# Past keys turned by VectorE in 32x32 blocks and moved by transfers inside the chip, in the attention stage of a decoder step

## What is computed

```python
def stick_breaking(q, k, v, bias, q_offset):
    z = jnp.einsum('bqhd,bkhd->bhqk', q.astype(f32), k.astype(f32)) * (HD_B ** -0.5)
    z = z + bias.astype(f32)[None, :, None, None]
    mask = jnp.arange(Lk)[None, :] < (q_offset + jnp.arange(Lq))[:, None]
    u = jnp.where(mask, jax.nn.log_sigmoid(-z), 0.0)
    rev_excl = lax.cumsum(u, axis=3, reverse=True) - u
    A = jnp.where(mask, jnp.exp(jax.nn.log_sigmoid(z) + rev_excl), 0.0)
    return jnp.einsum('bhqk,bkhd->bqhd', A, v.astype(f32))

past_k = cache_k[page_table].reshape(Bs, -1, H_B, HD_B)
past_v = cache_v[page_table].reshape(Bs, -1, H_B, HD_B)
```

## Time and profile before

| | |
|---|---|
| median of three runs | 1518.87 us |
| profiled execution, its time | 1517.85 us |
| its span | 1516.1 us |
| PE busy over the span | 1463.3 us, 97% |
| DVE, ACT, POOL busy | 75%, 51%, 21% |
| attention stage | from about 794 to 1099 us |

### The profile page before, as it was taken

How to read it: one execution, slowest core, us unless ns; L and a number is a source line. 1 busy time by engine, 2 the same in 40 slices (tenths; PEclk the granted TensorE clock), 3 DMA queues, 4 the chain that set the end, 5 groups by cost and what they waited for, 6 DMA issues and landing times.

```text
span 1516.1 us, 33061 instructions
## 1 busy us (share of the span) xinstructions
PE 1463.3 (97%) x13048; PEld 1391.0 (92%) x13048; DVE 1140.3 (75%) x1855; ACT 776.6 (51%) x1192; POOL 320.0 (21%) x307
## 2 busy tenths in 40 slices
PE   8999999999999999999998888888899999999998
PEld 8999999989999999999997777777699999999998
DVE  7866666668998989889726666666679989899753
ACT  6544444436754636455514555554557546364543
POOL 3000000002322323223141111111243223223221
PEclk9999999999999999999999999999999999999999
DMA  5133333223787786876426554553247777877721
GB/s 189 57 87 86 86 86 86 86 87 93 154 175 166 159 182 149 170 168 147 125 84 210 169 175 162 169 167 112 72 105 153 171 170 157 172 160 163 171 84 63
DMA packets 237716, 205.83 MB, mean 136 GB/s; under 512 B 8268, under 2 KB 224404, under 8 KB 237588
## 3 DMA queue, kind: packets, MB, share of 16 engines
q1 hardware_dynamic: 151346, 147.34, 30.9%
q0 software_dynamic: 68160, 47.20, 20.0%
q10 hardware_dynamic: 18082, 9.48, 2.3%
HBM read 192.19 MB, written 11.80 MB: 135 GB/s over the span
## 4 chain that ended last, share of the span: by engine, by line
PE 88%; DVE 5%; issue 4%; ACT 2%; DVEq 0%; DMA 0%; ACTq 0%
PE acc L2771 21%; PE acc L3095 19%; PE pMO L3095 12%; PE pL L3095 12%; PE acc L3195 5%; PE acc L3032 2%; PE pL L2892 1%; PE acc L3302 1%; PE pMO L3262 1%; PE acc L3318 1%; PE pMO L2961 1%; PE acc L3483 1%; PE acc L3291 1%; DVE pg L2544 1%; PE pMO L3249 1%
## 5 line engine op out<-in xcount | busy, mean ns | idle before, releaser
L654 POOL TENSOR_TENSOR wlo<-wraw,whi 128x512 fp32r<-128x512 f32 x40 | 56.2, 1433 | 455.2 <-ACT whi L768 455.2
L2771 PE MATMUL acc<-xa_hi,whi 128*128 128x288 f32 x544 | 125.2, 311 | 0.6 <-issue 0.6
L854 ACT ACTIVATE hi<-wraw 128x1024 fp32r<-128x1024 f32 x60 | 63.7, 1062 | 106.5 <-DVE wraw L1976 106.2
L2771 PE MATMUL acc<-xa_hi,wlo 128*128 128x288 f32 x544 | 116.6, 296 | 0.0
L837 ACT ACTIVATE hi<-wraw 128x1024 fp32r<-128x1024 f32 x60 | 63.7, 1061 | 102.8 <-PE acc L3095 102.6
L2771 PE MATMUL acc<-xa_lo,whi 128*128 128x288 f32 x544 | 116.2, 295 | 0.0
L3095 PE MATMUL acc<-X_lo,hi 128*128 128x288 f32 x384 | 113.4, 295 | 0.0
L3095 PE MATMUL acc<-X_hi,lo 128*128 128x288 f32 x384 | 113.4, 295 | 0.0
L3095 PE MATMUL acc<-X_hi,hi 128*128 128x288 f32 x384 | 113.2, 295 | 0.0
L1991 DVE TENSOR_TENSOR lo<-wraw,hi 128x1024 fp32r<-128x1024 f32 x60 | 73.4, 1223 | 41.9 <-ACT hi L837 41.9
L3095 PE MATMUL acc<-H_hi,hi 128*128 128x288 f32 x336 | 99.4, 296 | 1.3 <-DVE lo L1997 1.3
(11 more groups left out here) (513 smaller groups left out, 4943.8 us busy)
## 6 DMA issues: line engine op xcount, KB each, us to landing
wraw<-in_w_up_dram SPq DMA_DIRECT2D x64, 512.0 KB, 6.8
wraw<-in_w_down_dram SPq DMA_DIRECT2D x64, 512.0 KB, 6.2
Kp<-in_cache_k_dram SPq DMA_DIRECT2D x32, 512.0 KB, 4.0
Vp<-in_cache_v_dram SPq DMA_DIRECT2D x32, 512.0 KB, 5.6
wraw<-in_w_in_a_dram SPq DMA_DIRECT2D x30, 512.0 KB, 5.1
wraw<-in_w_up_dram POOLq DMA_DIRECT2D x32, 256.0 KB, 4.9
S_even<-in_w_up_dram POOLq DMA_DIRECT2D x32, 256.0 KB, 7.0
S_odd<-in_w_up_dram POOLq DMA_DIRECT2D x32, 256.0 KB, 8.1
```

Source lines behind the costliest of these rows:

```text
L654: ins = pool.tensor_tensor(wlo[s][:, k:k + 2, :], wraw[s][:, k:k + 2, :], whi[s][:, k:k + 2, :].bitcast(F32), ALU.subtract)
L854: act.activation(blocks4(hi31), by_depth(G % 2)[:, 0], ACT.Copy).then_inc(piece_hi, 1)
L2771: last = pe.matmul(acc[a][:, hf, 0:HALF], w[s][:, k, a * P:(a + 1) * P], x[k][:, hf * HALF:(hf + 1) * HALF], start=(k == 0 and n == 0), st ...
```

## The change

PE's `t_fill` and both `t_copy` go. Instead DVE turns a whole page at once in 32x32 blocks, `keys_turned(s, g)`, into a buffer `KX`, one for two pages. A 32x32 block is then still on the wrong 32 partitions; SP puts it right with `keys_moved(s, h)`, 16 transfers from `KX` to `KT` for each half of the past, each of 32 partitions by 512 elements (64 KB). `past_logits` waits for these and reads `KT` in pieces of 32. `keys_turned` for pages 0 and 2 waits until the moves before have landed, since `KX` is one buffer, and `keys_moved` waits until `past_logits` has read the half of `KT`.

The bank `TB` now also takes the transposed values and every second of the transposed weights (`ABANK = [pM, TB, pM, TB, pM]`), `pO` takes the sums and values of the new tokens, which stood in `ZB`. `fg` shrinks to two halves of 512. The order of a turn is written anew on every engine: on ACT `t_copy` drops out, `new_copies` comes after `gates(j, 2)`, `past_gates` and `attn_out` come earlier; SP's loop over j is unrolled. The core of the diff:

```diff
@@ -176,17 +176,19 @@
+                 ("KX", [P, 4, NPAIR, 2, 32], F32)])
         (KT, sgS, fS, pS, ATp, pastO, newE, newO, QB, Oc, kvn, sN, fN, pN, dN, AN, qnew, At0) = arena(
-            xa_at, [("KT", [P, NPAIR, 2, P], F32), ("sgS", [P, 512], F32), ("fS", [P, 512], F32), ("pS", [P, 513], F32),
...
+        N_MOVE = 16 * 16
@@ -525,9 +527,17 @@
                 page = sp.value_load(pt[0:1, bass.ds(4 * s + g, 1)], min_val=0, max_val=cache_k.shape[0] - 1)
-                wait(sp, T_full, 8 * s + 2 * g - 2)
+                wait(sp, k_turned, 4 * s + g - 1)
                 sp.dma_start(Kp[:, g % 2, :], cache_k[bass.ds(page, 1)].rearrange("a p h d -> p (a h d)")
                              ).then_inc(kp_landed[g % 2], 16)
+
+            def keys_moved(s, h):
+
+                sp.wait_ge(k_turned, 4 * s + 2 * h + 2)
+                wait(sp, zS_full, 2 * s + h)
+                for a in range(4):
+                    for b in range(4):
+                        sp.dma_start(KT[32 * b:32 * b + 32, a], KX[32 * a:32 * a + 32, b]).then_inc(k_moved, 16)
@@ -556,15 +566,19 @@
             def pages_and_weights(j, weights, more_pages):
-                kv_store(j)
-                key_page(j + 1, 2)
-                key_page(j + 1, 3)
-                value_pages(j + 1)
                 if more_pages:
                     key_page(j + 2, 0)
                     key_page(j + 2, 1)
+                kv_store(j)
+                keys_moved(j + 1, 1)
+                value_pages(j + 1)
                 if weights:
                     weights(0)
+                if more_pages:
+                    keys_moved(j + 2, 0)
+                    key_page(j + 2, 2)
+                    key_page(j + 2, 3)
+                if weights:
                     weights(1)
@@ -580,13 +594,18 @@
             sp.wait_ge(unit_done, U_OB)
+            keys_moved(0, 0)
             value_pages(0)
+            keys_moved(0, 1)
             key_page(1, 0)
             key_page(1, 1)
+            keys_moved(1, 0)
+            key_page(1, 2)
+            key_page(1, 3)
@@ -2450,8 +2455,19 @@
+            def keys_turned(s, g):
+
+                dve.wait_ge(kp_landed[g % 2], 32 * s + 16 * (g // 2) + 16)
+                if g % 2 == 0:
+                    wait(dve, k_moved, N_MOVE * (2 * s + g // 2))
+                dve.transpose(KX[:, :, :, g % 2, :].rearrange("p b j k -> p j b k"),
+                              Kp[:, g % 2, :].rearrange("p (j b k) -> p j b k", b=4, k=32)).then_inc(k_turned, 1)
+
             dve.wait_ge(n_rs, 2 * n_norm["mix1"] + 2)
             for m in range(NB):
+                if m == NB - 2:
+                    keys_turned(0, 0)
+                    keys_turned(0, 1)
                 dve.wait_ge(unit_done, U_Q + m + 1)
                 dve.tensor_tensor(qT[:, m, :].rearrange(tok2, a=2), accv(m % 2), t2v(rstd), ALU.mult).then_inc(acc_free[m % 2], 1)
                 if m < 4:
@@ -2592,38 +2597,54 @@
-            def pair(j, first):
+            def pair(j, first, more):
                 if first:
                     k_low(0)
                     q_low(0)
+                mask(j, 0)
                 k_rows(j)
-                mask(j, 0)
+                products(j, 0, 0)
+                new_rows(j)
+                new_mask(j)
...
                     past_out_even(0)
                     past_out_odd(0)
-                t_copy(j + 1, 1)
-                new_rows(j)
-                new_mask(j)
-                group(j, 0)
-                past_store(j)
                 mask(j, 1)
+                weights(j, 0, 1)
+                if first:
+                    past_store(0)
+                    keys_turned(1, 2)
+                    keys_turned(1, 3)
                 new_products(j)
-                t_copy(j + 1, 3)
-                queries(j + 1)
-                group(j, 1)
+                products(j, 1, 0)
                 mask(j, 2)
+                products(j, 1, 1)
+                kv_copy(j + 1, 0)
+                weights(j, 1, 0)
+                weights(j, 1, 1)
                 new_out(j)
-                kv_copy(j + 1, 0)
-                t_copy(j + 1, 5)
-                group(j, 2)
-                t_copy(j + 1, 7)
-                k_low(j + 1)
+                for hh in range(2):
+                    products(j, 2, hh)
+                for hh in range(2):
+                    weights(j, 2, hh)
                 past_products(j + 1)
                 past_weights(j + 1)
-                kv_copy(j + 1, 1)
+                if more:
+                    queries(j + 2)
+                    keys_turned(j + 2, 0)
+                    keys_turned(j + 2, 1)
+                k_low(j + 1)
                 q_low(j + 1)
+                if more:
+                    keys_turned(j + 2, 2)
+                    keys_turned(j + 2, 3)
                 past_out_even(j + 1)
                 past_out_odd(j + 1)
+                kv_copy(j + 1, 1)
 
             def ob_low(m):
@@ -2672,18 +2701,22 @@
             kv_copy(0, 0)
+            keys_turned(1, 0)
+            keys_turned(1, 1)
+            dve.wait_ge(row_chain, 3)
+            queries(1)
             past_products(0)
             past_weights(0)
@@ -3264,48 +3301,28 @@
             def past_logits(s, h2):
-                pe.wait_ge(Ta_free, 4 * s + 2 * h2 + 2)
-                pe.wait_ge(Td_free, 4 * s + 2 * h2 + 2)
+                pe.wait_ge(k_moved, N_MOVE * (2 * s + h2 + 1))
                 pe.wait_ge(QB_ready, 4 * s + 4)
-                wait(pe, n_dve, 6 * s)
+                wait(pe, fin_free, 2 * s)
@@ -3331,46 +3348,44 @@
                 if first:
-                    past_values(0)
+                    past_transposed(0)
                 else:
                     past_finish(j)
...
+                if first:
+                    past_values(0)
                 new_rows(j)
+                values_transposed(j)
+                fill(2, 3)
+                logits(j, 1)
                 if first:
+                    fill(3, 4)
                     past_finish(0)
-                t_fill(j + 1, 1)
-                fill(1, 3)
-                values_transposed(j)
-                t_fill(j + 1, 2)
-                logits(j, 1)
-                fill(3, 4)
-                t_fill(j + 1, 3)
+                else:
+                    past_logits(j + 1, 0)
+                    fill(3, 4)
+                fill(4, 5)
+                if first:
+                    past_logits(1, 0)
+                weights_transposed(j, 0)
+                weights_transposed(j, 1)
                 new_sums(j)
-                weights_transposed(j, 0)
-                fill(4, 6)
+                logits(j, 2)
+                fill(5, 8)
+                past_logits(j + 1, 1)
                 new_values(j)
-                weights_transposed(j, 1)
-                logits(j, 2)
-                past_logits(j + 1, 0)
-                t_fill(j + 1, 4)
-                fill(6, 8)
-                t_fill(j + 1, 5)
                 weights_transposed(j, 2)
                 fill(8, 9)
-                t_fill(j + 1, 6)
                 weights_transposed(j, 3)
                 fill(9, 10)
-                t_fill(j + 1, 7)
+                weights_transposed(j, 4)
                 fill(10, 11)
-                past_logits(j + 1, 1)
+                weighted(j)
                 fill(11, 12)
-                weights_transposed(j, 4)
+                past_transposed(j + 1)
                 fill(12, 14)
-                weighted(j)
-                past_transposed(j + 1)
+                past_values(j + 1)
                 fill(14, 16)
-                past_values(j + 1)
 
             def ob_prompt_part(u, k):
```

More of the change, by code:

```diff
@@ L588, in _ @@
             pages_and_weights(0, lambda a: kv_weights(3, a), True)
-            with sp.Fori(1, NPAIR - 3) as j:
+            for j in range(1, NPAIR - 3):
                 pages_and_weights(j, lambda a: kv_weights(j + 3, a), True)
@@ L1386, in new_copies @@
                     act.activation(newE[rows, bass.ds(j, 1), :].rearrange("p a t -> p (a t)"),
-                                   ZB[rows, SMP * hh:SMP * hh + SMP], ACT.Copy).then_inc(n_act, 1)
+                                   pO[rows, SMP * hh:SMP * hh + SMP], ACT.Copy).then_inc(n_act, 1)
             def gates(j, g):
@@ L1394, in gates @@
                     z = pL[:, hh, 0:GW[g]]
-                    act.activation(fg[:, hh, cols], z, ACT.Sigmoid, scale=-SCALE, bias=bias_neg[:, bass.ds(2 * j + hh, 1)]
+                    wait(act, p_done, 6 * j + (2 * g + hh - 1 if g else 0))
+                    act.activation(fg[:, hh, 0:GW[g]], z, ACT.Sigmoid, scale=-SCALE, bias=bias_neg[:, bass.ds(2 * j + hh, 1)]
                                    ).then_inc(s_done, 1)
@@ L2552, in weights @@
                 dve.tensor_tensor(sg[:, hh, cols], sg[:, hh, cols], pg[:, hh, 0:GW[g]], ALU.mult).then_inc(a_done, 1)
-            def group(j, g):
-                for hh in range(2):
-                    products(j, g, hh)
```

(46 more changed lines are left out.)

140 lines of the change are left out of this document (51 added, 89 removed).

## The result

The kernel after takes 1626.78 us (median of 4 runs, 1625.72 to 1627.56) against 1518.72 (4 runs, 1518.13 to 1518.95): ratio 1.0712, interval 1.0693 to 1.0730. Slower, as forecast (0.88), but 49 us beyond the forecast and just past the range's end of 1625. The profiled execution has a span of 1624.7 against 1516.1.

The account below looks back on a forecast made before the run. PE was taken to bound the kernel, holding 88% of the chain. Start +25.6, five turns +35.5 and turn 6 -2.0 gave +59.1 us, so 1578 against a profiled 1517.85 and a median 1.0 above it; range 1532 to 1625.

Parts of the forecast that it names:

- The circle: Attention turn: SP's two move batches, page loads and DVE's turnings lie on PE's path; turn 42.7 against 35.6 us.
- cheap issues: Rival: issues of moves at 0.37 us, everything else as forecast; turn 37.6, total about 1539; chance 0.16.
- a faster kernel: Rival: the moves hold nobody up and PE leads again; 1480 at 0.1 us an issue; chance 0.08.
- small pieces: Rival: transfers in pieces under 2 KB, or not on all DMA engines; about 1690; chance 0.05.
- step 2: Turn: 16 moves and landing, 8.5 + 1.4, to 18.1; PE waits 3.9 before `past_logits(j+1, 1)`.
- Step 5: Turn: 16 moves 8.5 us, first page landed 4.1 later, to 39.5.
- Step 6: Turn: two page turnings 2.4 us and two `past_out` 0.8, to 42.7, the next `past_finish`.
- The clock: PE, once a turn behind the long stop: 3.5 us at half speed lose 1.7; ends nothing and 3.4.
- Step 1: Turn: PE from `past_finish` to the end of `past_logits(j+1, 0)`, 8.2 us including 1.7 for PE's slower clock.
- step 3: Turn: `past_logits` 1.0, `new_values` 0.4, DVE's `new_out` through `past_weights` 2.4 and 2.0; 5.8 us, to 23.9.
- step 4: Turn: `queries` 0.6 us and two page turnings on DVE 2.4, to 26.9.
- dear steps: Rival: turning 2.44 us, page landing 5.6, issue 0.60; turn 51.4, total 1637; chance 0.09.

Follow-up runs that it names:

- the last orders: The orders of `no gaps`, changed against the run with the new start, with two page loads right ahead of each batch of moves: 1515.58 us.
- the last run: `no gaps` with two moves a batch (one on SP, one on POOL) instead of 16, keys on wrong partitions: 1505.12 us, ratio 0.9920.
- no gaps: Against the run with the new start, orders alone: fills ahead of weights_transposed, group 2's weights earlier, start reordered: 1515.58 us, ratio 0.9982.
- the run with the new start: Kernel after with turnings, page loads and moves reordered, eight moves each on SP and POOL, start ordered anew: 1517.73 us, ratio 0.9995.

## Why the prediction was right in its cause and short in its size

The circle was right: both batches of moves lie on PE's path, the waits stand where they were forecast, before `past_finish` and before `past_logits(j+1, 1)`, and the load of page 2 is what DVE waits for. Both waits were larger, 11.7 and 5.5 us where 9 and 4 stood. The turning was right too (1.22 forecast, 1.233 measured), and so were the landing of a move (1.9 forecast, 2.0 measured) and of a page (4.0 and 4.1). The estimate from the Trainium skill (VectorE: DVE Perf Modes, section The three transpose paths), eight times its 311 ns for a 128x128 bf16 transpose, was 2.5 us a page and 1608. The trace disagrees: a page of four-byte elements took 1.233, half of it; the 128x128 form itself is in no run. 1608 is nearer to the 1627 only because other terms were too small. The rivals of cheap issues, of a faster kernel and of small pieces fell.

What failed were terms of the sum, the price of an issue first. In the turn from 990.39 on and the batch before it:

- The issue of a move, steps 2 and 5: 0.53, measured 0.63 from one start to the next, so 10.04 a batch and not 8.5. That is 3.1 of the 7 us by which a turn was too short. I took a store from 64 partitions as the nearest row, and of it the duration of one. But what counts in a row is the step from start to start, and the trace of before had it: the two `kvn` stores of a turn begin 0.57 to 1.01 apart (0.64 at 895.93, where each lasts 0.53), and the second lasts 0.56 in the median. A move lasts 0.59 and the next begins 0.04 behind it. The upper end of 0.60 was too low as well, and the cheapest issue of the trace was 0.33 (the value pages), not 0.34.
- Step 5 left out the reading of the page number, which stands on SP between the last move and the next load: 980.94 to 981.69, 0.75.
- Step 6 took both pages as landed; the second was turned after a further wait of 1.48.
- The clock, taken as 3.5 us at half speed and 1.7 lost, once a turn: it falls behind both stops, to 0.50 from before `past_finish` at 990.39 to about 996.5, and from 1010.4 to about 1017. Step 1 took 8.65 against 8.2, step 3 7.1 (960.9 to 968.0) against 5.8; in it `past_logits` lasts 1.94 instead of 1.07.
- Together, with the forecast in brackets, step 2 took 11.7 (9.9), step 4 2.9 (3.0), step 5 14.6 (12.6) and step 6 4.9 (3.2); with steps 1 and 3 this is 49.8 against the 42.7 forecast, for a mean of 49.55.
- The start: `past_finish` of turn 1 at 891.2, not 878.5. Four batches before it are 6.2 of the 12.7. By place, 5.2 had gathered at `logits(0, 0)` (831.75 for 826.5), 2.7 more at `past_logits(1, 1)` (861.84 for 853.9) and 4.8 behind it. What isn't the price of issues was not separated; page numbers, second pages and the clock are at work there too.
- Turn 6, 37.4 against 33.6, has the second batch and the clock in it.

The rival "dear steps" gave the better time, 1637, for a wrong reason: it had the turning at 2.44. Its price for an issue, 0.60, was near. By the prediction's own rate, 2.4 us of the sum for 0.01 us of an issue, the 0.10 that was missing is 24 of the 49 missing microseconds. The other 25 are the smaller terms above.

"If PE stayed the bound, a turn would shrink to about 29.5" wasn't reached in any version. With two issues a batch and the best order it took 32.8, and the three turns of these at a granted clock of 1.00 took 32.5. PE was busy for 28.2 of them, so its work would have allowed 29.5; the 4.3 us between are waits, mostly for DVE's `sg` (8.5 us in the three turns) and for the moves (2.4).

What stays open is why an issue from and to on-chip memory takes SP 0.59 and POOL 0.50; no run looks inside one. Nor was a third queue (ACT's) tried, nor a batch of four moves, nor the last orders with the page loads out of the way of the moves.

## What to carry to other kernels

Before work is taken from the busiest engine and given to transfers, count the issues that stand one behind the other between a producer and its consumer, at the step from one start to the next of issues of the same kind, and put what is read ahead of each (a page number) into the count. A queue's load says little about it: SP was issuing for some 30 of 50 us and held PE all the same, and moving a handful of lines gave back 79 of 108 us. Once the issues are short or hidden, look at the landing again, since a landing time read in one order (2.0 here) need not hold in another (5.0). Work that waits for a transfer must not stand in front of work that the bounding engine waits for.

## What the runs showed that I had not expected

- An issue costs the same for 32 partitions of 2 KB, 32 of 1 KB and 128 of 512 B (median 591, 591, 601 ns, 0.63 apart in a row); one move of 128 partitions with 8 KB each was issued in 0.51. But it isn't a constant: in the last run, where the four stores of the new rows stand right behind two page loads and a large move, the last of them took 1.78 us in the median, against 0.60 in `no gaps`.
- POOL issues the same moves in 0.50, though its other transfers take 0.78 to 1.7 in this program. They land when SP's do: after 2.2 in the orders of the kernel after, after 5 in the last ones.
- A turning of a 128x1024 page with four-byte elements takes 1.233 us, the same as a two-input operation of that size.
- PE's clock can fall where PE has only short stops, and costs a turn about 2 us even where PE is busy for 31 of 35. In the run with the new start it was at 0.50 from about 974.5 to 981, behind stops of 1.24 and 0.60 us; one turn later, behind 1.23, 0.60 and 0.61, it stayed at 1.00. What decides is not shown. Runs of `no gaps` spread over 1510 to 1519 with mean clocks of 0.980 to 0.989, those of the kernel before beside it over 1516 to 1520 with 0.997 to 0.999; that the one comes from the other is likely, not shown.
